# One unit of shares turned at a time, keys and values before queries, weight splits before the heads, and the latents' norms among the Hyena transforms

## The chip, the cores and the metric

The kernel runs on one core of one Trainium2 chip. The metric is the device time of one execution in microseconds (us); the median of several executions is given. The core has TensorE (PE, matmuls and transposes into PSUM), VectorE (DVE), ScalarE (ACT), GpSimd (POOL, here only an issuer of DMAs) and SyncE (SP, the issuer of the weight stream). Each engine works through its own queue in order and waits on semaphores.

## The reference

Two layers over 256 context and 256 latent tokens of width 1024. Each layer mixes tokens and then channels. Token mixing, cut to what matters here:

```python
hy, pool, cq, ckv, kpe = split(h @ w_in)          # 768, 256, 384, 256, 32 columns
y_hy   = hyena_mix(hy)                            # short convolution, long convolution by transforms, gates
y_pool = pool_mix(pool)                           # four window means, a 64x64 matmul for each group
k, v   = split(rmsnorm(ckv) @ w_ukv); k_pe = rope(kpe)
q      = rope(rmsnorm(cq) @ w_uq)                 # 8 heads of 64 + 32
att    = softmax(q @ k.T * SM_SCALE) @ v          # context sees context, latents see both
x      = x + gate * (concat(y_hy, y_pool, att) @ w_out)
```

Channel mixing is a dense SwiGLU in layer 0 and eight experts of SwiGLU, two for each token, in layer 1. In layer 1 only the latent tokens go on past the keys and values. All is float32; the large matmuls are made of three fp32r products of high and low parts.

## The kernel before, in words

Activations lie transposed, 128 channels by 512 tokens (256 context, 256 latent) in a tile. The order on each engine is written out by hand: PE, ACT, DVE, SP and POOL each have a program with a function for each stage (`project_in`, `hyena`, `pooling`, `latents`, `attention`, `project_out`), and all hand over through one counting semaphore for each engine (`pe_done`, `act_done`, `dve_done`); `after("name")` is the count at which a named step is done.

**Weight stream.** SP loads 1 MB granules in the order of `stream_plan()` into a ring of three `raw` buffers (a granule's load waits until the one three places before it has been used or split). For each granule ACT casts `w_hi` (L1102) and DVE subtracts `w_lo` (L1595), through `upto(g)` at places chosen by hand; there are three slots. Granules `("ada", 0, i)` hold modulation weights; PE uses them raw in `plain(n)` (two granules for each n), ACT saves the row (`save_row`), PE turns it (`turn`), DVE adds the bias (`bias_mod`). In layer 0 `plain(4)` to `plain(9)` are strewn through the mixing.

**Stages around the change, PE's order in layer 0.** `hyena`: transposes of z, eight matmuls against the transform bases (L617), `plain(4)` (in layer 1 `shift_rows`), wait for the products Y of DVE, inverse transform y (L630, L631). `pooling`: `turn(4)`, `plain(5)`, window matmuls d (L647), group matmuls yp (L656), with ACT's copies dT between. `latents`: `turn(5)`, `plain(6)`, transposes of the normed latents cq (L670) and ckv (L677) and of the rotary key (L683), `turn(6)`, `plain(7)`, the queries of eight heads (L695), keys (L703), values (L709), `turn(7)`, `plain(8)`. DVE computes the latents' sums of squares (L1849, L1852), the reciprocal (L1856), the scaling (L1860, L1863), the rotary key (L1870 to L1874), the drains of the queries (L1882 to L1891: one head is one PSUM bank, 256 context columns and 256 latent columns) and the copies of the values (L1895), in this order and behind all of Hyena. ACT drains the transposed latents (L1290, L1296), writes the rotary key into all heads' keys (L1301, eight copies) and drains the keys (L1309). POOL loads `w_uq`, `w_ukv` and both rotary tables in one go after the end of Hyena.

**Attention.** A unit is 128 query rows of one latent head against 512 keys, or one context head with both its query tiles against 256 keys. Layer 0 has 8 context and 16 latent units, layer 1 has 16 latent units. For each unit: PE scores (L728) into one of three banks; DVE maximum (L1908); ACT exponential with its sum (L1330) into one of four `prob` buffers; DVE reciprocal and scaling, the shares (L1917, L1921); PE transposes (L741); ACT copy to `probT` (L1345); for each pair of heads PE multiplies with the values (L755), ACT and DVE split the result (L1352, L1929). A latent head's `turn_p(n, half)` fills a bank with the blocks of one half of the keys for both query tiles, and so takes from both units of the head:

```python
for t in range(2):
    own = first[n] + t if s else u
    eng.wait_ge(dve_done, after(f"ps {l} {own}"))
```

Scores are issued three units ahead (`ahead_to(first[n] + half + 3)`). At heads `out_splits = {0: (4, 9, 12), 1: (1, 3, 5)}` ACT and DVE split the next granule of `w_out` inside the loop. `project_out` (L435 to L437) follows.

## Time and profile before

| | us |
|---|---|
| median of three runs | 1751.36 (1748.71 to 1754.73) |
| the profiled execution, its own time | 1748.31 |
| its span | 1746.5 |
| PE busy | 1631.9 (93%) |
| DVE busy | 1299.3 (74%) |
| ACT busy | 894.0 (51%) |
| share of the chain that ended last: PE, DVE, ACT | 63%, 16%, 5% |

The span is cut by the profile into 40 slices; the mixing of layer 0 lies in slices 3 to 7 (up to about 284 us, then its output projection), that of layer 1 in slices 18 to 21 (about 786 to 890 us). Busy time says how long an engine had work in flight, the chain says what the end waited for. The granted clock is TensorE's, as a share of 2.4 GHz; it has two levels, 1.2 and 2.4 GHz, and a stretch's figure is a mean over both.

### The profile page before, as it was taken

Reading aid. Unit: us, or ns where it says so; the run is one execution under the profiler, and the core shown is the slowest. Engines: PE = TensorE matmul, PEld = TensorE weight load, DVE = VectorE, ACT = ScalarE, POOL = GpSimd, SP = SyncE. Lnnn points to the kernel's source line nnn. Section 1 sums busy time; section 2 is a strip of 40 time slices with the busy share of each in tenths; the row PEclk is TensorE's granted clock in tenths of the full one; section 3 lists DMA queues with packets and bytes.
Section 4 is the critical chain, followed back from the end, with each engine's and each line's share of the span. In section 5 each row is a group of like instructions: output and inputs, shape, how many; then the busy total and the mean of one; then the engine's idle time right before and its main releaser. Section 6 shows DMA issues by size and latency. Waiting matters only on the chain.

```text
span 1746.5 us, 19442 instructions
## 1 busy us (share of the span) xinstructions
PE 1631.9 (93%) x7404; PEld 1269.4 (73%) x7404; DVE 1299.3 (74%) x1769; ACT 894.0 (51%) x1019; POOL 14.7 (1%) x31
## 2 busy tenths in 40 slices
PE   5998978899999999797888999999999999999996
PEld 3774446777888888685377778888787878878775
DVE  3825454688787765846447989898988989888897
ACT  3322264332222222432557776677777776777774
POOL 1000000000000000000000000000000000000000
PEclk8997999899999999898998999999999999999999
DMA  9225131354445553131026889899999999999993
GB/s 392 73 95 212 61 115 57 134 205 157 161 158 213 195 215 145 46 118 68 26 87 265 338 348 352 342 354 359 344 335 337 360 358 353 345 346 365 345 347 115
DMA packets 56004, 403.49 MB, mean 231 GB/s; under 512 B 6433, under 2 KB 6465, under 8 KB 8801
## 3 DMA queue, kind: packets, MB, share of 16 engines
q1 hardware_dynamic: 53712, 387.47, 59.1%
q0 software_dynamic: 2192, 14.70, 2.2%
q8 instruction: 62, 1.02, 0.2%
q14 instruction: 38, 0.30, 0.0%
HBM read 401.10 MB, written 1.05 MB: 230 GB/s over the span
## 4 chain that ended last, share of the span: by engine, by line
PE 63%; DVE 16%; ACT 5%; issue 3%; DVEq 0%; ACTq 0%
PE PS L435 18%; PE PS L437 18%; PE PS L436 18%; DVE w_lo L2234 5%; ACT w_hi L1472 3%; DVE w_lo L1595 1%; DVE arena L1608 1%; PE PS L986 1%; PE PS L728 1%; DVE small L1908 1%; PE PS L755 1%; DVE XT L1955 1%; DVE arena L1921 1%; DVE hT_lo L1743 1%; PE PS L741 1%
## 5 line engine op out<-in xcount | busy, mean ns | idle before, releaser
L2234 DVE TENSOR_TENSOR w_lo<-arena,w_hi 128x2048 fp32r<-128x2048 f32 x132 | 301.7, 2291 | 44.0 <-ACT w_hi L1472 44.0
L2234 DVE TENSOR_TENSOR w_lo<-raw,w_hi 128x2048 fp32r<-128x2048 f32 x129 | 295.0, 2291 | 32.7 <-ACT w_hi L1472 32.2
L1472 ACT CAST w_hi<-arena 128x2048 fp32r<-128x2048 f32 x132 | 251.6, 1909 | 47.3 <-PE PS L437 47.3
L1472 ACT CAST w_hi<-raw 128x2048 fp32r<-128x2048 f32 x129 | 246.9, 1916 | 44.3 <-PE PS L437 44.3
L435 PE MATMUL PS<-hT_hi,w_hi 128*128 128x512 f32 (+1 forms) x576 | 217.7, 378 | 11.3 <-DVE hT_lo L1743 9.9
L436 PE MATMUL PS<-hT_lo,w_hi 128*128 128x512 f32 (+1 forms) x576 | 214.8, 373 | 0.0
L437 PE MATMUL PS<-hT_hi,w_lo 128*128 128x512 f32 (+1 forms) x576 | 214.7, 373 | 0.0
L435 PE MATMUL PS<-w_hi,hT_hi 128*128 128x512 f32 (+1 forms) x448 | 178.3, 398 | 0.3 <-DVE w_lo L2234 0.3
L437 PE MATMUL PS<-w_hi,hT_lo 128*128 128x512 f32 (+1 forms) x448 | 174.6, 390 | 0.0
L436 PE MATMUL PS<-w_lo,hT_hi 128*128 128x512 f32 (+1 forms) x448 | 173.6, 388 | 0.0
L1595 DVE TENSOR_TENSOR w_lo<-raw,w_hi 128x2048 fp32r<-128x2048 f32 (+1 forms) x54 | 122.4, 2266 | 30.0 <-ACT w_hi L1102 29.9
L435 PE MATMUL PS<-w_hi,f_hi 128*128 128x512 f32 x352 | 140.6, 399 | 3.5 <-DVE f_lo L2241 3.5
L436 PE MATMUL PS<-w_lo,f_hi 128*128 128x512 f32 x352 | 139.0, 395 | 0.0
L437 PE MATMUL PS<-w_hi,f_lo 128*128 128x512 f32 x352 | 138.7, 394 | 0.0
L435 PEld LDWEIGHTS PS<-hT_hi,w_hi 128*128 128x128 f32 x576 | 110.6, 192 | 34.3 <-DVE hT_lo L1743 11.7
L435 PE MATMUL PS<-w_hi,odd_hi 128*128 128x512 f32 x336 | 135.3, 403 | 0.0
L1102 ACT CAST w_hi<-raw 128x2048 fp32r<-128x2048 f32 (+1 forms) x54 | 102.3, 1894 | 60.9 <-PE PS L437 53.3
L437 PE MATMUL PS<-w_hi,odd_lo 128*128 128x512 f32 x336 | 131.8, 392 | 0.0
L436 PE MATMUL PS<-w_lo,odd_hi 128*128 128x512 f32 x336 | 131.0, 390 | 0.0
L437 PEld LDWEIGHTS PS<-hT_hi,w_lo 128*128 128x128 f32 x576 | 110.5, 192 | 18.7
L436 PEld LDWEIGHTS PS<-hT_lo,w_hi 128*128 128x128 f32 x576 | 110.7, 192 | 18.1
L1955 DVE SCALAR_TENSOR_TENSOR XT<-PS,mod,XT 128x256 f32<-128x256 f32 x200 | 85.0, 477 | 40.3 <-PE PS L437 39.9
(320 smaller groups left out, 2533.3 us busy)
## 6 DMA issues: line engine op xcount, KB each, us to landing
raw<-in_moe SPq DMA_DIRECT2D x132, 1024.0 KB, 6.4
arena<-in_moe SPq DMA_DIRECT2D x132, 1024.0 KB, 6.6
raw<-in_ffn SPq DMA_DIRECT2D x33, 1024.0 KB, 4.8
raw<-in_dot SPq DMA_DIRECT2D x28, 1024.0 KB, 4.9
raw<-in_ada SPq DMA_DIRECT2D x17, 1024.0 KB, 6.7
raw<-in_out SPq DMA_DIRECT2D x8, 1024.0 KB, 4.8
raw<-in_inb SPq DMA_DIRECT2D x8, 960.0 KB, 4.8
raw<-in_ina SPq DMA_DIRECT2D x5, 1024.0 KB, 5.2
```

The costliest lines, as they stand in the source:

```text
L435: mm(out, s_hi, m_hi, start=start, stop=False)
L436: mm(out, s_hi, m_lo, start=False, stop=False)
L437: return mm(out, s_lo, m_hi, start=False, stop=stop)
L728: i = mm(o[:, q], qT[0:96, h, P * t:P * t + P], KT[0:96, h, 0:512 if s else 256], start=True, stop=True)
L741: i = nc.tensor.transpose(o[:, 256 * b + P * t:256 * b + P * t + P], prob[:, own % 4, at:at + P], ident[:, :])
L755: i = mm(o[VD * j:VD * j + VD, 0:256], V[:, b, VD * (h + j):VD * (h + j) + VD], probT[:, (2 * pair + j) % 4, b, :], start=b == 0, stop=b = ...
L986: last = nc.tensor.transpose(PS[:, 2, P * f:P * f + P], hh[:, s % 2, P * f:P * f + P], ident[:, :])
L1102: nc.scalar.copy(w_hi[:, slot[n], 0:w], raw_at(n)[:, 0:w]).then_inc(act_done, 1)
L1472: nc.scalar.copy(w_hi[:, x_slot(j), :], x_raw(n)).then_inc(x_hi, 1)
L1595: v.tensor_tensor(w_lo[:, slot[n], 0:w], raw_at(n)[:, 0:w], w_hi[:, slot[n], 0:w].bitcast(F32), ALU.subtract).then_inc(dve_done, 1)
L1955: v.scalar_tensor_tensor(out=XT[:, k, q], in0=o[:, q], scalar=mod[:, l, j + k, s:s + 1], in1=XT[:, k, q], op0=ALU.mult, op1=ALU.add).then_ ...
L2234: v.tensor_tensor(w_lo[:, x_slot(j), :], x_raw(NGR * (i % 2) + j), w_hi[:, x_slot(j), :].bitcast(F32), ALU.subtract).then_inc(x_lo, 1)
```

## The change

- PE, `hyena`: the window matmuls d move in front of the wait for Y. `pooling` starts with yp; `turn(4)` and `plain(5)` follow it.
- DVE, `hyena`: begins with `latent_sums` (sums of squares and the rotary key), then z times its bias; after Y comes `scale_latents`; both splits of Hyena's output come after both of its gates. ACT takes the square roots right after its copies of zT, and the splits' high parts after pooling's.
- PE, `latents`: ckv is turned before cq, `turn(5)` and `plain(6)` come after the transposes, then keys, values, queries. Queries are made in pairs of heads of one stream, one bank for a pair, 256 columns for each matmul instead of 512 in layer 0; DVE drains a context pair with one instruction and a latent pair with four 512 columns wide.
- The splits of three `w_out` granules leave the attention loop: ACT splits the first before the keys' drains and the next two after them, DVE the first before the values' copies and the others after query pairs 1 and 3. In the stream of layer 0 `("ada", 0, 16..19)` move behind the third of them.
- Attention: a unit is turned by itself, all its four blocks, as soon as its own shares are there; scores are issued four ahead; a `prob` buffer is free when its own unit was turned; `probT` is written in runs of 128.
- POOL: `w_ukv` is loaded once the forward transforms are done, `w_uq` and the query table once Hyena's gates are; the key table is loaded once.

```diff
@@ stream_plan
-            plan += [("ada", 0, i) for i in range(2 * BEFORE, 20)]
-        plan += [("out", l, i) for i in range(4)]
+            plan += [("ada", 0, i) for i in range(2 * BEFORE, 16)]
+        plan += [("out", l, i) for i in range(3)]
+        if l == 0:
+            plan += [("ada", 0, i) for i in range(16, 20)]
+        plan.append(("out", l, 3))
-        dT = A(2048, 2, 512)
+        dT = A(17544, 2, 512)
-        out_splits = {0: (4, 9, 12), 1: (1, 3, 5)}
@@ PE, latents
-                    turn(0, 5)
-                    plain(6)
+                for k in range(KKV):
+                    o = bank(f"ckvT {l} {k}")
...
                 if l == 0:
+                    turn(0, 5)
+                    plain(6)
                     turn(0, 6)
                     plain(7)
...
-                for h in range(HEADS):
-                    o = bank(f"q {l} {h}")
-                    for k in range(KQ):
-                        i = mm(o[:, sp], wuq[:, k, h, :], cqT[:, k, sp], start=k == 0, stop=k == KQ - 1)
...
+                heads = attention_plan(streams)[0]
+                for pair in range(len(heads) // 2):
+                    o = bank(f"q {l} {pair}", pair)
+                    for j in range(2):
+                        s, h = heads[2 * pair + j]
+                        for k in range(KQ):
+                            i = mm(o[:, 256 * j:256 * j + 256], wuq[:, k, h, :], cqT[:, k, 256 * s:256 * s + 256],
+                                   start=k == 0, stop=k == KQ - 1)
@@ PE, attention
-                def turn_p(n, half):
+                def turn_p(u):
+                    n, j = units[u]
                     s, h = heads[n]
-                    u = first[n] + half
+                    eng.wait_ge(dve_done, after(f"ps {l} {u}"))
                     o = bank(f"pT {l} {u}", 3 + u % 3)
-                    for t in range(2):
-                        own = first[n] + t if s else u
-                        eng.wait_ge(dve_done, after(f"ps {l} {own}"))
-                        for b in range(2):
-                            at = P * (2 * half + b) if s else 256 * t + P * b
-                            i = nc.tensor.transpose(o[:, 256 * b + P * t:256 * b + P * t + P],
-                                                    prob[:, own % 4, at:at + P], ident[:, :])
+                    for b in range(4):
+                        at = P * b if s else 256 * (b // 2) + P * (b % 2)
+                        to = P * b if s else 256 * (b % 2) + P * (b // 2)
+                        i = nc.tensor.transpose(o[:, to:to + P], prob[:, u % 4, at:at + P], ident[:, :])
...
-                ahead_to(2)
+                ahead_to(3)
...
-                        ahead_to(first[n] + half + 3)
-                        turn_p(n, half)
+                        ahead_to(first[n] + half + 4)
+                        turn_p(first[n] + half)
@@ ACT, latents
                 if l == 0:
                     save_row(0, 7)
+                upto(gindex[("out", l, 0, 0)])
                 for pr in range(4):
...
+                upto(gindex[("out", l, 2, 0)])
@@ ACT, attention
-                        m = units[u - 4][0]
-                        eng.wait_ge(pe_done, after(f"pT {l} {first[m] + heads[m][0]}"))
+                        eng.wait_ge(pe_done, after(f"pT {l} {u - 4}"))
...
-                    nc.scalar.copy(probT[:, n % 4, 2 * half:2 * half + 2, :],
-                                   bank_of(f"pT {l} {u}").rearrange("p (b q) -> p b q", q=256)).then_inc(act_done, 1)
+                    q = P if heads[n][0] else 256
+                    to = probT[:, n % 4, :, P * j:P * j + P] if heads[n][0] else probT[:, n % 4, 0:2, :]
+                    nc.scalar.copy(to, bank_of(f"pT {l} {u}").rearrange("p (b q) -> p b q", q=q)).then_inc(act_done, 1)
...
-                    if n in out_splits[l]:
-                        upto(gindex[("out", l, out_splits[l].index(n), 0)])
@@ DVE, new: latent_sums (first in hyena) and scale_latents (after Y), the instructions of latents before
+            def latent_sums(l, streams):
+                for t in range(NT):
+                    eng.wait_ge(act_done, after(f"Bs {l} 1 {t}"))
...
+                eng.wait_ge(*loaded["rope keys"])
...
+            def scale_latents(l, streams):
+                eng.wait_ge(act_done, after(f"stdq {l}"))
+                v.reciprocal(small[:, 24:32], small[:, 24:32]).then_inc(dve_done, 1)
...
@@ DVE, latents
+                upto(gindex[("out", l, 0, 0)])
                 for t in range(NT):
                     eng.wait_ge(pe_done, after(f"v {l} {t}"))
                     v.tensor_copy(V[:, t, :], bank_of(f"v {l} {t}")).then_inc(dve_done, 1)
...
+                for pair in range(len(heads) // 2):
+                    eng.wait_ge(pe_done, after(f"q {l} {pair}"))
+                    if heads[2 * pair][0] == 0:
+                        v.tensor_scalar(qT[0:96, pair, :], o[0:96, :], SM_SCALE, None, ALU.mult).then_inc(dve_done, 1)
...
+                    else:
+                        v.tensor_scalar(qT[0:64, pair, :], o[0:64, :], SM_SCALE, None, ALU.mult).then_inc(dve_done, 1)
+                        v.tensor_tensor(qT[64:96, pair, :], o[64:96, :], ropeq[64:96, :], ALU.mult).then_inc(dve_done, 1)
+                        v.tensor_tensor(qtmp[64:96, :], o[96:128, :], ropeq[96:128, :], ALU.mult).then_inc(dve_done, 1)
...
+                        v.tensor_tensor(qT[64:96, pair, :], qT[64:96, pair, :], qtmp[64:96, :], ALU.add).then_inc(dve_done, 1)
...
+                    if pair in (1, 3):
+                        upto(gindex[("out", l, 1 + pair // 2, 0)])
@@ POOL
-                eng.wait_ge(dve_done, after(f"hyena {l}"))
-                eng.wait_ge(pe_done, after(f"y {l} 1"))
+                if l == 0:
+                    load("rope keys", (A(20224, 128), io["ropek"]))
                 eng.wait_ge(pe_done, after(f"zT {l} 1"))
-                eng.wait_ge(act_done, after(f"mixhi {l} 1"))
-                load(f"mla {l}", (A(7936, 3072), io["wuq"][l]), (A(11008, 2048), io["wukv"][l]), (A(19712, 512), io["ropeq"]),
-                     (A(20224, 128), io["ropek"]))
+                eng.wait_ge(pe_done, after(f"Zs {l} 1"))
+                load(f"kv {l}", (A(11008, 2048), io["wukv"][l]))
+                eng.wait_ge(dve_done, after(f"yh {l} 1"))
+                load(f"q {l}", (A(7936, 3072), io["wuq"][l]), (A(19712, 512), io["ropeq"]))
```

## Rows read from the trace of the kernel before

**Rows 1.** The page's first part: busy time, share of the span, instructions.

```profile
PE 1631.9 (93%) x7404; PEld 1269.4 (73%) x7404; DVE 1299.3 (74%) x1769; ACT 894.0 (51%) x1019; POOL 14.7 (1%) x31
```

**Rows 2.** Stages: us; busy of PE, PEld, DVE, ACT, POOL; PEclk; DMA share; GB/s.

```profile
134.00:216.20 82.20, 75.50 (x290) 39.96 (x289) 38.83 (x105) 20.72 (x36) 2.16 (x4) 0.88 0.37 139
216.20:284.50 68.30, 53.23 (x285) 30.28 (x281) 39.82 (x92) 41.60 (x101) 0.00 (x0) 0.95 0.29 108
786.30:842.70 56.40, 45.46 (x171) 30.61 (x172) 29.80 (x82) 15.75 (x33) 2.14 (x4) 0.88 0.14 53
842.70:889.70 47.00, 35.19 (x162) 17.85 (x160) 28.34 (x55) 27.65 (x55) 2.11 (x4) 0.93 0.22 79
```

**Rows 3.** The chain that ended last, layer 1's attention: start, duration, engine and line.

```profile
857.54 1.81 ACT w_hi L1102
859.37 2.29 DVE w_lo L1595
861.66 0.60 DVE small L1908
...
877.03 0.69 DVE small L1908
877.83 0.50 DVE arena L1921
878.37 0.44 PE PS L741 x2
878.81 0.86 PE PS L728 x2
879.67 0.44 PE PS L741 x4
880.11 1.90 PE PS L755 x16
```

**Rows 4.** Groups by form, layer 1's mixing: busy, mean ns, idle before.

```profile
L1330 ACT ACTIVATE arena<-PS,small 128x512 f32<-128x512 f32 x16 | 11.0, 690 | 12.0 <-DVE small L1917 5.8 <-PE PS L755 5.6 <-issue 0.6
L695 PE MATMUL PS<-arena 128*128 128x256 f32 x48 | 11.6, 406 | 0.0
L695 PEld LDWEIGHTS PS<-arena 128*128 128x128 f32 x48 | 9.9, 209 | 1.6
L741 PE MATMUL PS<-ident,arena 128*128 128x128 f32 x64 | 12.1, 296 | 10.9 <-DVE arena L1921 10.9
L1301 ACT COPY arena<-PS 32x512 f32<-32x512 f32 x8 | 3.9, 579 | 0.2 <-PE PS L683 0.2
```

**Rows 5.** PE in order of time, layer 0: start, duration, idle before.

```profile
139.26 1.22 PE L630 MATMUL PS<-arena 128*128 128x256 f32 x2 [3.30 <-DVE arena L1808]
...
152.02 7.12 PE L647 MATMUL PS<-arena 128*64 128x256 f32 x32
...
169.96 3.87 PE L670 MATMUL PS<-ident,arena 128*128 128x128 f32 x12 [2.26 <-DVE arena L1860]
...
177.04 1.92 PE L445 MATMUL PS<-raw,cpad 128*32 128x512 f32 x16
```

**Rows 6.** PE in order of time, layer 1.

```profile
808.04 1.83 PE L670 MATMUL PS<-ident,arena 128*128 128x128 f32 x6 [5.92 <-DVE arena L1860]
...
827.18 8.80 PE L703 MATMUL PS<-arena 128*128 128x512 f32 x16 [3.35 <-DVE arena L1889]
```

**Rows 7.** DVE in order of time, both layers' first product Y, and a query drain.

```profile
130.78 0.42 DVE L1798 TENSOR_TENSOR arena<-PS,arena 128x256 f32<-128x256 f32 x1 [27.39 <-PE PS L617]
...
788.30 0.42 DVE L1798 TENSOR_TENSOR arena<-PS,arena 128x256 f32<-128x256 f32 x1 [19.85 <-PE PS L617]
...
815.25 0.42 DVE L1887 TENSOR_TENSOR arena<-PS,arena 32x256 f32<-32x256 f32 x1
```

**Rows 8.** DMA issues from 145 to 185 us: size, median time to landing.

```profile
raw<-in_ada SPq DMA_DIRECT2D x6, 1024.0 KB, 6.4
...
arena<-in_wukv POOLq DMA_DIRECT2D x1, 1024.0 KB, 12.1
```

More of the change, by code:

```diff
@@ L623, in hyena @@
                     shift_rows()
+                eng.wait_ge(*loaded[f"pool {l}"])
+                for t in tiles_of(streams):
+                    eng.wait_ge(act_done, after(f"Bs {l} 0 {t}"))
+                for g in range(4):
+                    o = bank(f"d {l} {g}")
+                    for s in streams:
+                        for t in range(2):
+                            i = mm(o[0:GROUP, 256 * s:256 * s + 256], Bm[:, 2 * s + t, GROUP * g:GROUP * g + GROUP],
+                                   pm[:, g, t, :], start=t == 0, stop=t == 1)
+                    i.then_inc(pe_done, 1)
+                    did(f"d {l} {g}")
                 eng.wait_ge(dve_done, after(f"Y {l}"))
@@ L635, in pooling @@
             def pooling(l, streams):
-                if l == 0:
-                    turn(0, 4)
-                    plain(5)
-                eng.wait_ge(*loaded[f"pool {l}"])
                 sp = span(streams)
-                for t in tiles_of(streams):
-                    eng.wait_ge(act_done, after(f"Bs {l} 0 {t}"))
-                for g in range(4):
-                    o = bank(f"d {l} {g}")
-                    for s in streams:
-                        for t in range(2):
-                            i = mm(o[0:GROUP, 256 * s:256 * s + 256], Bm[:, 2 * s + t, GROUP * g:GROUP * g + GROUP],
-                                   pm[:, g, t, :], start=t == 0, stop=t == 1)
-                    i.then_inc(pe_done, 1)
-                    did(f"d {l} {g}")
                 for pair in range(2):
@@ L1246, in hyena @@
                             did(f"zTs {l} {ct}", f"read zT {l} {ct}")
+                eng.wait_ge(dve_done, after(f"ssq {l}"))
+                act(small[:, 24:28], small[:, 16:20], ACT.Sqrt, bias=epsb[:, 0:1], scale=1.0 / QL).then_inc(act_done, 1)
+                did()
+                act(small[:, 28:32], small[:, 20:24], ACT.Sqrt, bias=epsb[:, 0:1], scale=1.0 / KVL).then_inc(act_done, 1)
+                did(f"stdq {l}")
                 if l == 0:
@@ L1253, in hyena @@
                         did("shift row", f"read shift {half}")
-                for ct in range(2):
-                    eng.wait_ge(dve_done, after(f"yh {l} {ct}"))
-                    nc.scalar.copy(hT_hi[:, ct, sp], ytmp[:, ct, sp]).then_inc(act_done, 1)
-                    did(f"mixhi {l} {ct}")
             def pooling(l, streams):
                 sp = span(streams)
-                if l == 0:
-                    save_row(0, 5)
                 for g in range(4):
@@ L1275, in pooling @@
                     did(f"mixhi {l} {2 + pair}")
+                for ct in range(2):
+                    eng.wait_ge(dve_done, after(f"yh {l} {ct}"))
+                    nc.scalar.copy(hT_hi[:, ct, sp], ytmp[:, ct, sp]).then_inc(act_done, 1)
+                    did(f"mixhi {l} {ct}")
+                if l == 0:
+                    save_row(0, 5)
             def latents(l, streams):
                 sp = span(streams)
[L1279 to L1283 removed]
                 if l == 0:
                     save_row(0, 6)
+                for k in range(KKV):
+                    eng.wait_ge(pe_done, after(f"ckvT {l} {k}"))
+                    o = bank_of(f"ckvT {l} {k}")
+                    a = PAR["kvg"][0] + k
+                    act(ckvT[:, k, :], o, ACT.Copy, scale=par[:, l, a:a + 1]).then_inc(act_done, 1)
+                    did(f"ckvTs {l} {k}", f"read ckvT {l} {k}")
                 for k in range(KQ):
@@ L1338, in soften_to, with save_turned @@
                         done += 1
-                def save_turned(n, half):
-                    u = first[n] + half
+                def save_turned(u):
+                    n, j = units[u]
                     eng.wait_ge(pe_done, after(f"pT {l} {u}"))
@@ L1357, in attention @@
                         soften_to(first[n] + half + 3)
-                        save_turned(n, half)
+                        save_turned(first[n] + half)
                     if l == 0 and n == 0:
@@ L1787, in hyena @@
             def hyena(l, streams):
                 sp = span(streams)
+                latent_sums(l, streams)
+                b0 = PAR["hyb"][0]
+                for ct in range(2):
+                    eng.wait_ge(pe_done, after(f"zT {l} {ct}"))
+                    z = uc[:, 2 + ct, sp]
+                    v.tensor_scalar(z, z, par[:, l, b0 + ct:b0 + ct + 1], None, ALU.mult).then_inc(dve_done, 1)
+                    did()
                 if l == 0:
```

157 lines of the change are left out of this document (67 added, 90 removed).

## The prediction

> **What bounds the kernel now.** I read the page first, then the stages around the change, then the chain, then single engines in order of time. PE is busy for 93% of the span [rows 1], but the mixing of both layers is where that is not so. From 134.0 to 216.2 us (layer 0, inverse transform to the first scores) PE is busy for 75.5 of 82.2 us at a mean clock of 0.88; in attention it is busy for 53.2 of 68.3; in layer 1 for 45.5 of 56.4 and for 35.2 of 47.0 [rows 2]. The reader is to see that neither DVE nor ACT fills those stretches (39.8 and 41.6 of 68.3, 28.3 and 27.7 of 47.0): they are bound by waits between engines, not by one engine. The chain says which: in layer 1's attention it runs maximum, share, transposes, score and round again, and through the two splits of a granule, 1.81 on ACT and then 2.29 on DVE [rows 3]. PE waited 10.9 us for shares before its transposes there [rows 4]. Ahead of attention PE waits for Y (3.30 us) and for the scaled latents (2.26 in layer 0, 5.92 in layer 1), and in layer 1 for the drain of the queries before the keys (3.35) [rows 5, 6].
>
> **Layer 0 ahead of attention.** A mean clock of 0.88 between the levels of 0.5 and 1 puts 24% of 82.2 us, 19.7 us, at the lower level. If the 6.7 idle us lie in it, 13.0 busy us ran at half speed and 6.5 were lost: the work at full clock is 69.0 us. The change removes none of it. It puts d, 7.1 us [rows 5], where the 3.30 us wait was. Y itself gets later: in front of it DVE now has six sums of squares for the queries and keys and more. But DVE sat idle for 27.39 us before Y [rows 7], and the last latent arrives less than 6 us before Y starts; I put the delay, with the key table's load, at 2.5 us, which 7.1 us of d cover (without them PE would wait 5.8). The scaled latents are ready before y ends, so the 2.26 us wait goes. The clock should then stay up. New waits: ACT's `save_row` 6 stands ahead of the drains of ckv, so `turn(6)` waits some 1.4 us for row and bank; and `plain(7)`'s second granule is loaded only when the first of `plain(6)` is used. A granule takes 6.4 us to land [rows 8]; between lie half of `plain(6)`, `turn(6)` with its wait, and half of `plain(7)` (1.9 us a `plain` [rows 5]), some 4.2 us: 2.2 us of waiting. The gap of 0.8 us in yp for ACT's copies stays. Sum: 69.0 + 1.4 + 2.2 + 0.8 = 73.4, a gain of 8.8; bounds 0 (the waits in ACT's queue give it all back) and 13.2 (no wait at all). The weights of the keys, 12.1 us to land [rows 8], are asked for about 35 us before their use, so their load is hidden; if it were not moved it would end the wait of the keys.
>
> **Queries in pairs.** In layer 0, 24 matmuls of 512 columns (two instructions each) become 48 of 256: as many columns, twice the weight loads. Layer 1 already does it so: 48 instructions of 256 columns in 11.6 us with 9.9 us of weight loads beside them [rows 4], a part of it at the lower clock. Loads and streams overlap there, so I price this at nothing; if they did not, 48 more loads at 0.209 us would be 10.0 us.
> The Trainium skill ("TensorE: Matmul & The Clock Gate", Part 3) says that a weight load overlaps a running matmul only where the row group differs, which speaks against this edit; by that rule queries in layer 1 should have taken the sum of both rows, 21.5 us, and they took 11.6, so the trace disagrees. By it the whole change would gain 10.0 us less.
>
> **Attention, layer 0.** PE's prices at full clock are 0.86 for a score, 0.44 for four transposes and 1.90 for the values of a latent pair, which is four units [rows 3]: 1.78 a unit, 28.4 for 16. A context unit has as many columns in its score and its turn and half as many value blocks: 1.78 too, 14.2 for 8. With `turn(8)` and `plain(9)` (about 2.8) that is 45.4 of the 68.3 us. The question is whether the other engines now let PE do it. DVE needs 0.60 to 0.69 for a maximum and 0.50 for a scaling; over layer 1's stretch (28.34 - 3 x 2.29) / 16 = 1.34 us a unit [rows 2, 3]. ACT needs (27.65 - 3 x 1.81) / 16 = 1.39. Both are under 1.78. The loop of waits is: exponential of u (0.69 and its sum), share (0.2 + 0.5), then the maximum of u+2 behind it in DVE's queue (0.6), then the exponential of u+2: some 2.4 us for two units, 1.2 a unit, also under 1.78. Before, `turn_p` of the first half waited for the share of the second unit, and the score that feeds the next pair stood behind it; now a unit waits for itself alone, with scores three further ahead and a `prob` buffer freed a unit earlier. The three splits, 3 x (1.81 + 2.29) of stalled queues [rows 3], leave the loop for a stretch in which PE is busy with values and queries and DVE for only a part. I add 0.9 us for the last share's way into the last value matmul, 1.3 us for `plain(9)`'s last granule, which now starts its load only when `plain(8)` begins, and 2.3 us of small gaps: 49.9 us, a gain of 18.4. Bounds: 0, and 22.9 (45.4 reached).
>
> **Layer 1 ahead of attention.** Of 56.4 us PE's full-clock work is between 38.7 and 44.2 (13.5 us at the lower level, with none or all of the 10.9 idle us in it [rows 2]); I take the middle, 41.5, plus 1 us, so the queries end at 828.8. DVE's sums again lie in its idle time before Y (19.85 us [rows 7]). The waits of 5.92 and 3.35 go. But what is late next is DVE: four query pairs, each 4 x 0.72 = 2.9 us (a 512-wide operation at 0.69 [rows 3]; a 256-wide one takes 0.42 [rows 7]), against 2.6 us a pair on PE, and two splits of 2.29 among them, the last right ahead of the first maximum. From the first pair on PE, 828.8 - 3 x 2.6 = 821.0, it is 11.6 + 4.6 = 16.2 us to the first maximum, 837.2, against 843.7 (the 842.7 of the stretch's end, one score and a handover later): 6.5 us earlier. PE waits for 8 us in between, and the wait will take its clock down for a while.
>
> **Attention, layer 1.** From the first maximum it is about 2.9 us to the first exponential's end. Three scores are done by then: 28.4 - 2.6 = 25.8 us of PE's work remain, plus 0.9 at the tail, 2.0 for the low clock after the wait (half of some 4 us), 1.5 of gaps: the last value matmul ends at 837.2 + 33.1 = 870.3 instead of 889.7, a gain of 19.4 for the layer, bounds 0 and 24. The output projections, the dense layer and the experts keep their work and order; their stalls are elsewhere. ACT's eight key copies (3.9 us [rows 4]) end before the third key matmul needs a bank; I price them at nothing.
>
> **Sum.** 8.8 + 18.4 + 19.4 = 46.6 us. I take off 2.6 for waits not foreseen: 44. The profiled execution took 1748.3 us (span 1746.5), so 1704.3; the median of the three runs is 3.1 above it: 1707.4.
>
> **Rivals.**
> 1. *The attention loop stays bound by handovers.* DVE and ACT are in order; a maximum queued behind a share that waits for ACT can make a unit take 2.3 us instead of 1.78 (against about 2.8 now). Then half of attention's 31.3 us (18.4 and 12.9) is had: gain 8.8 + 6.5 + 15.7 = 31 us, about 1720. For it: DVE waited for scores and ACT for maxima in the same stretch. Against: none of the loops adds up to 1.78. Chance 0.16.
> 2. *The queues ahead of attention take back what the order gives.* ACT's `save_row` 6 ahead of the ckv drains, the splits ahead of the values' copies, `plain` granules behind splits: the 15.3 us of both front stretches shrink to nothing: 31 us, about 1720. Chance 0.10.
> 3. *Weight loads show.* 48 more at 0.209 us, 10 us: 1717. Chance 0.04.
> 4. *Slower.* The copy into `probT` in runs of 128 (same 128x512 elements) would have to make ACT the bound: the 46.6 us of gain over 40 units, and the 1.78 us they are paced by, mean 2.9 us of ACT a unit, and so a copy of 2.1 us where a whole unit of ACT with its exponential now takes 1.39. From there on the change costs. No row shows such runs; 1755 to 1760 then. Chance 0.02.
> 5. *All waits gone*, over 54 us: under 1697. Chance 0.04.
> The forecast itself, 1697 to 1716, has 0.64.
>
> **Range.** Rivals 1 to 3 reach 1720 to 1726 (with half of 2 on top of 1); so 1697 to 1726. A measurement tells about 0.3%, 5 us, from no change: faster 0.95, same 0.02, slower 0.03.
>
> **What would show it.** In the profile after: PE without the wait before L630 and the clock near 1 up to the queries; the L741 group's idle time before it down from 10.9 us to 3 or less in layer 1; no L1102 or L1595 between L1908s; score starts 1.8 us apart; in layer 1 an idle PE of some 8 us after the third score. It would be wrong if L741 still waits for L1921 in every unit, if ACT's L1345 grew beyond 0.6 us, or if PE waits for a granule at `plain(7)` to `plain(9)` for more than a few us.

## The result, and the profile after

| | us |
|---|---|
| before, median of four runs | 1751.71 (1748.71 to 1754.73) |
| changed kernel, median of four runs | 1708.59 (1707.65 to 1709.24) |
| ratio, 95% interval | 0.9755 (0.9739 to 0.977) |
| predicted | 1707.4, range 1697 to 1726 |
| profiled execution after, its span | 1708.7, 1706.8 |

The medians differ by 43.1 us, the profiled executions by 39.6; that of before lies 3.4 us under its own median, which is the rest. The stages below are read against the 39.6.

Line numbers below are those of the kernel profiled, so one step has other numbers after than in [rows] and in some experiments. The page after, its first part and the engines of the chain that ended last; they answer to [rows 1]:

```profile
PE 1618.1 (95%) x7452; PEld 1273.2 (75%) x7452; DVE 1294.3 (76%) x1733; ACT 891.7 (52%) x1019; POOL 14.1 (1%) x30
...
PE 76%; DVE 15%; ACT 5%; issue 3%; DMA 1%; SPq 0%; DVEq 0%; ACTq 0%
```

PE is busy for 14 us less although it runs 48 instructions more: less of its work fell into time at half the clock (the mean granted clock of the two profiled executions is 0.977 against 0.97). Its share of the chain grew from 63% to 76%, so the waits were what went. The same stages as in [rows 2] (up to the first score, and attention; columns as there):

```profile
134.80:210.60 75.80, 71.16 (x337) 44.96 (x336) 37.32 (x65) 23.62 (x36) 1.60 (x3) 0.93 0.51 191
210.60:259.20 48.60, 47.31 (x284) 29.70 (x280) 34.89 (x93) 35.36 (x98) 0.00 (x0) 1.00 0.22 87
761.70:808.00 46.30, 42.40 (x171) 28.22 (x172) 23.91 (x51) 20.69 (x36) 1.62 (x3) 0.96 0.24 86
808.00:850.20 42.20, 32.65 (x162) 18.28 (x160) 29.41 (x61) 22.02 (x52) 2.12 (x4) 0.84 0.14 53
```

In layer 0 the front went from 82.2 to 75.8 us and attention from 68.3 to 48.6, where PE is now busy for 97% at a clock of 1.00. In layer 1 the front is 10.1 us shorter up to the first score, but attention only 4.8: a wait moved over the border. From the first maximum on, the split that I used, the front gained 2.6 us and attention 12.4.

PE in order of time, layer 0's front (start, duration, idle before):

```profile
136.67 7.12 PE L635 MATMUL PS<-arena 128*64 128x256 f32 x32
143.72 0.70 PE L645 MATMUL PS<-arena 128*128 128x256 f32 x2
...
164.01 1.94 PE L449 MATMUL PS<-raw,cpad 128*32 128x512 f32 x8 [2.45 <-DMA raw<-in_ada]
167.33 1.84 PE L469 MATMUL PS<-sel,rows 128*128 128x2 f32 x8 [1.39 <-ACT arena L1296]
169.10 3.64 PE L449 MATMUL PS<-raw,cpad 128*32 128x512 f32 x16
```

The window matmuls (L635) run straight into y (L645): the 3.30 us wait of [rows 5] is gone. The two waits behind them are the granule and `turn(6)`, and what runs after them is at half speed: 16 of L449 took 3.64 us where they take 1.92 at full clock. DVE in front of Y, which had idled for 27.39 us there [rows 7], now waits 5.13 us for the key table; by these rows that wait, and not the sums of squares, is what makes Y later:

```profile
131.79 0.19 DVE L1809 TENSOR_TENSOR arena<-arena 128x32 f32<-128x32 f32 x1 [5.13 <-DMA arena<-in_ropek]
...
133.45 0.42 DVE L1848 TENSOR_TENSOR arena<-PS,arena 128x256 f32<-128x256 f32 x1
```

Groups by form, the queries of layer 0:

```profile
L716 PE MATMUL PS<-arena 128*128 128x256 f32 x96 | 20.9, 379 | 0.0
...
L716 PEld LDWEIGHTS PS<-arena 128*128 128x128 f32 x96 | 18.2, 190 | 2.9 <-issue 0.5
```

96 instructions with 18.2 us of weight loads beside them in 20.9 us; before, 48 of 512 columns took 20.87 (all of L695 in layer 0). Groups by form, attention of layer 0 and then, last two rows, the mixing of layer 1, against L741 in [rows 4]:

```profile
L749 PE MATMUL PS<-ident,arena 128*128 128x128 f32 x96 | 14.2, 273 | 0.0
L1356 ACT COPY arena<-PS 128x512 f32<-128x512 f32 x24 | 14.1, 593 | 8.8 <-PE PS L749 8.7
...
L737 PE MATMUL PS<-arena 96*128 96x512 f32 x32 | 19.0, 684 | 8.6 <-ACT arena L1339 7.7 <-DVE arena L1913 0.9
...
L749 PE MATMUL PS<-ident,arena 128*128 128x128 f32 x64 | 10.3, 291 | 0.0
```

No transposes wait for shares any more. The copy in runs of 128 takes 0.59 us. What is left in layer 1 is one idle of 7.7 us ahead of the fourth score. PE and then DVE in order of time there, against [rows 6, 7]:

```profile
779.93 1.96 PE L698 MATMUL PS<-arena 128*128 128x512 f32 x4 [1.40 <-ACT arena L1302]
783.80 7.12 PE L698 MATMUL PS<-arena 128*128 128x512 f32 x12 [1.91 <-ACT arena L1309]
...
819.57 2.04 PE L737 MATMUL PS<-arena 96*128 96x512 f32 x2 [7.70 <-ACT arena L1339]
```
```profile
792.67 0.69 DVE L1899 COPY arena<-PS 128x512 f32<-128x512 f32 x1 [4.67 <-PE PS L704]
...
800.41 0.68 DVE L1909 TENSOR_SCALAR arena<-PS 64x512 f32<-64x512 f32 x1 [1.90 <-PE PS L716]
...
806.17 2.29 DVE L1603 TENSOR_TENSOR w_lo<-raw,w_hi 128x2048 fp32r<-128x2048 f32 x1
...
814.26 2.29 DVE L1603 TENSOR_TENSOR w_lo<-raw,w_hi 128x2048 fp32r<-128x2048 f32 x1
816.58 1.29 DVE L1930 TENSOR_REDUCE small<-PS 128x1 f32<-128x512 f32 x2
```

The reader is to see three things: the keys wait for ACT twice; DVE idles for 4.67 us and more ahead of the query drains (L1909); and then it makes two splits (L1603) in the one stretch where everyone waits for it. The three experiments on mends below follow from these rows.

### The profile page after: what moved, and what is told of

It reads as the page before. It is cut to its first block, busy times and chain, and to the rows that moved or that the text cites. A ratio compares the mean times of both kernels' runs of the same rounds, so it can differ in the third digit from the quotient of the medians.

```text
span 1706.8 us, 19495 instructions
## 1 busy us (share of the span) xinstructions
PE 1618.1 (95%) x7452; PEld 1273.2 (75%) x7452; DVE 1294.3 (76%) x1733; ACT 891.7 (52%) x1019; POOL 14.1 (1%) x30
## 3 DMA queue, kind: packets, MB, share of 16 engines
HBM read 401.03 MB, written 1.05 MB: 236 GB/s over the span
## 4 chain that ended last, share of the span: by engine, by line
PE 76%; DVE 15%; ACT 5%; issue 3%; DMA 1%; SPq 0%; DVEq 0%; ACTq 0%
PE PS L439 20%; PE PS L441 20%; PE PS L440 20%; DVE w_lo L2254 6%; ACT w_hi L1480 3%; PE PS L737 2%; DVE arena L1616 1%; DVE w_lo L1603 1%; PE PS L993 1%; PE PS L762 1%; PE PS L749 1%; DMA arena<-in_ada 1%; PE PS L698 1%; PE PS L449 1%; PE PS L704 1%
## 5 line engine op out<-in xcount | busy, mean ns | idle before, releaser
L439 PE MATMUL PS<-hT_hi,w_hi 128*128 128x512 f32 (+1 forms) x576 | 217.6, 378 | 12.2 <-DVE hT_lo L1751 10.6
L1603 DVE TENSOR_TENSOR w_lo<-raw,w_hi 128x2048 fp32r<-128x2048 f32 (+1 forms) x54 | 122.3, 2266 | 34.8 <-ACT w_hi L1109 34.6
L439 PEld LDWEIGHTS PS<-hT_hi,w_hi 128*128 128x128 f32 x576 | 110.3, 191 | 34.7 <-DVE hT_lo L1751 12.4
```

Of the source, the lines that this page charges most:

```text
L439: mm(out, s_hi, m_hi, start=start, stop=False)
L1603: v.tensor_tensor(w_lo[:, slot[n], 0:w], raw_at(n)[:, 0:w], w_hi[:, slot[n], 0:w].bitcast(F32), ALU.subtract).then_inc(dve_done, 1)
```

## The experiments

Each was timed against the kernel before, whose medians in the four series were 1750.8, 1751.4, 1751.0 and 1751.4 us. "Layer 0 attention" is from the first score to the last value matmul's start, "layer 1" from the first transform to there; the changed kernel has 48.3 and 88.2 there, the kernel before 68.0 and 102.9. All stages are from one profiled execution each. In layer 1 twelve key matmuls, behind the same wait of 1.91 us, took 7.12 us in the profiles marked * and 5.42 in those marked + (last section); compare that column within a group, or take 1.7 us off the marked *.

| run | median, us | ratio (95%) | layer 0 attention | layer 1 |
|---|---|---|---|---|
| changed kernel | 1708.59 | 0.9755 (0.9739 to 0.977) | 48.3 | 88.2 * |
| halves, three ahead | 1730.58 | 0.9884 (0.9866 to 0.9902) | 61.2 | 95.2 + |
| splits inside | 1720.80 | 0.9831 (0.9815 to 0.9848) | 56.7 | 89.1 + |
| both | 1736.81 | 0.9917 (0.9897 to 0.9937) | 69.5 | 96.0 + |
| three ahead | 1717.10 | 0.9807 (0.9791 to 0.9824) | 53.8 | 89.9 * |
| halves, four ahead | 1709.38 | 0.9766 (0.975 to 0.9782) | 48.6 | 88.3 * |
| before + unit turning, four ahead | 1730.90 | 0.9889 (0.9873 to 0.9906) | 56.6 | 94.3 |
| before + four ahead | 1736.70 | 0.9918 (0.9902 to 0.9935) | 60.2 | 99.0 |
| windows behind y | 1713.91 | 0.9784 (0.9766 to 0.9801) | 48.3 | 88.6 * |
| splits among the values | 1702.57 | 0.9723 (0.9706 to 0.9741) | 48.3 | 81.7 + |
| key banks | 1705.18 | 0.9734 (0.9712 to 0.9757) | 48.3 | 82.3 |
| layer 0's front | 1705.10 | 0.9738 (0.9719 to 0.9756) | 48.3 | 85.9 + |
| all mends | 1698.95 | 0.9699 (0.9681 to 0.9718) | 51.1 | 78.7 |

### Which part of the change made the loop fast

**1. Halves, three ahead.**

```diff
-                    eng.wait_ge(dve_done, after(f"ps {l} {u}"))
+                    for t in range(2):
+                        own = first[n] + t if s else u
+                        eng.wait_ge(dve_done, after(f"ps {l} {own}"))
...
-                        ahead_to(first[n] + half + 4)
-                        turn_p(first[n] + half)
+                        ahead_to(first[n] + half + 3)
+                        turn_p(n, half)
```

> The changed kernel with the turning of the shares taken back alone: turn_p(n, half) fills a bank from both units of a latent head and waits for both shares, probT is written in runs of 256, a prob buffer is free only when the whole head was turned, scores are three units ahead. Keys and values first, the splits ahead of the heads and the mixing's order stay as changed. Theory (the wait for the second share makes the loop, and splits come on top of it): the larger part of attention's gain goes, some 12 us in layer 0 and 7 in layer 1, so about 1727; the transposes' idle time before them comes back in every head. Rival S (the splits in the loop were the stall, 3 x (1.81 + 2.29) = 12.3 us a layer): less than 5 us slower, up to 1713.

22.0 us slower; layer 0's attention is 13.0 us longer and layer 1 7.0 (8.7 with the keys at the same clock): near the theory's 12 and 7. PE there, for two heads (L750 are the transposes, L764 the values):

```profile
248.64 1.95 PE L764 MATMUL PS<-arena 128*64 128x256 f32 x16
...
253.02 0.44 PE L750 MATMUL PS<-ident,arena 128*128 128x128 f32 x2 [1.16 <-DVE arena L1945]
...
256.99 0.44 PE L750 MATMUL PS<-ident,arena 128*128 128x128 f32 x2 [0.80 <-DVE arena L1945]
...
258.66 1.95 PE L764 MATMUL PS<-arena 128*64 128x256 f32 x16
```

The second block of each head waits for the second unit's share: 10.02 us for four units.

**2. Splits inside the loop**, the stream's order of before with them.

```diff
+        out_splits = {0: (4, 9, 12), 1: (1, 3, 5)}
...
-                upto(gindex[("out", l, 0, 0)])
...
+                    if n in out_splits[l]:
+                        upto(gindex[("out", l, out_splits[l].index(n), 0)])
```

> The changed kernel with the three splits of w_out in each layer back inside the attention loop (and the stream's order of before, which goes with them); turning by the unit and everything else stay. Theory: each split holds ACT for 1.81 us and then DVE for 2.29, but with scores four ahead a part of it is covered: 2 to 3 us a split in the loop, less the 2 us that the DVE splits cost ahead of layer 1's first maximum; 8 to 12 us slower in all, 1717 to 1721. Rival S: 24.6 us less about 4 in front, so about 1729. Rival C (with per-unit turning the splits are covered by PE's own 1.78 us a unit): within 3 us of the changed kernel, or faster through layer 1's front.

12.2 us slower, at the edge of what the theory gave. In layer 0 the three splits cost attention 8.5 us. In layer 1 they cost 7.3 after the first maximum, but that maximum comes 48.5 us after the first transform instead of 54.9, so the layer as a whole differs by 0.9 us. Of the 6.3 us of the maximum 1.7 are the clock of the keys; with that taken off, the maximum moves by the 4.6 of two splits and the layer differs by 2.6. Out of the loop, most of what layer 1's splits cost had only been moved ahead of it.

**3. Both back.**

> The changed kernel with both taken back, turning by halves with scores three ahead and the splits inside the loop; keys and values first, queries in pairs and the mixing's order stay. Theory: all of attention's gain of 32 us goes and layer 1's front gains 2 to 4 by the splits it no longer holds: about 1738. If the two parts of the gain are separate causes, this is the sum of the two runs with one taken back; if each is enough to keep the loop slow, it is less than the sum.

28.2 us slower, against a sum of 34.2 for the two alone (the edit is both diffs above). In layer 0's attention they are separate causes (13.0 + 8.5 us; together 21.3). Of the 6.0 us by which the sum is missed a part lies ahead of attention: up to the first score layer 0 is 2.9 us shorter than in the changed kernel, against 0.0 and 0.7 in the two runs before. Why, and where the rest lies, was not found. Attention in layer 0 takes 69.5 us with both back, 68.0 before: queries in pairs and the rest of the change gave it nothing. This run is still 14.0 us faster than the kernel before, and that comes from the fronts: up to the first maximum layer 0 is 9.0 us shorter than before and layer 1 8.9.

**4. Three ahead**, turning by the unit.

```diff
-                ahead_to(3)
+                ahead_to(2)
...
-                        ahead_to(first[n] + half + 4)
+                        ahead_to(first[n] + half + 3)
```

> The changed kernel with scores three units ahead instead of four (ahead_to(2), then + 3); turning stays by the unit. Theory (the depth only hides jitter, the gain is in what turn_p waits for): 1 to 4 us slower, 1710 to 1713. Rival D (the depth carries the gain): over 10 us slower, since a unit's round through maximum, exponential and share is some 2.9 us and PE has 1.78 us of work a unit to put in front of it.

8.5 us slower, twice the theory's bound and under the rival's. So the depth is more than jitter.

**5. Halves, four ahead.** Experiment 1 with `ahead_to(3)` and `+ 4` left as they are in the changed kernel.

> The changed kernel with the turning by halves back, as in the first experiment, but scores four units ahead as changed. Taken back together they cost 22.0 us, the depth alone 8.5. Theory (each hides a part of the same round of maximum, exponential and share): turning alone costs 10 to 15 us, 1719 to 1724. Rival (where a half waits for the second unit's share, a fourth score ahead can't be used): as with three ahead, 1729 to 1731.

0.8 us slower than the changed kernel, which these measurements can't tell from no change. Both the theory and the rival were wrong: with a fourth score ahead it hardly matters whether a unit or a half is turned. One round of layer 0's loop, from one value group to the next (four units), takes in the four runs: 7.27 us as changed, 7.35 halves and four ahead, 7.86 units and three ahead, 10.02 halves and three ahead. Start times of the changed kernel (L762 the values, L737 a score):

```profile
239.74 1.95 PE L762 MATMUL PS<-arena 128*64 128x256 f32 x16
241.62 1.12 PE L737 MATMUL PS<-arena 96*128 96x512 f32 x2
242.58 0.60 PE L749 MATMUL PS<-ident,arena 128*128 128x128 f32 x4
...
247.01 1.95 PE L762 MATMUL PS<-arena 128*64 128x256 f32 x16
```

The programs say why: DVE takes the maximum of unit u+1 ahead of the share of unit u. With halves, the first transposes of a head need the share of u+1 and therefore the score of u+2. Three ahead, that is the last score issued, directly in front of them; four ahead, there is one more score between (0.86 us of PE), and units instead of halves give one more again. The count of scores between fits the two ends, none (10.02) and two (7.27). It doesn't explain the middle: both others have one, and one of them costs 8.5 us, the other 0.8. A half waits only once for two units, a unit each time; that this makes the difference was not tested.

**6. Unit turning and four ahead on the kernel before; 7. four ahead alone on it.**

> The kernel before with one part of the change alone: turn_p by the unit, scores four ahead, prob buffers freed by the unit, probT in runs of 128. Splits stay in the loop, queries ahead of keys, mixing as before. Theory (the parts act in the attention loop and nowhere else, so they give what they gave between the runs with both taken back and with the splits inside alone, 1736.8 - 1720.8 = 16.0): 16 us faster than the kernel before, about 1735. Rival (the gain depends on what stands ahead of attention): under 8 us.

> The kernel before with nothing changed but the depth: ahead_to(3) and + 4. Turning stays by halves, the splits in the loop, queries ahead of keys. Theory (DVE takes the maximum of unit u + 1 ahead of the share of unit u, so the first half of a head, which needs the share of u + 1, needs the score of u + 2, and with three ahead that is the last one issued, right in front of the transposes; a fourth score is work for PE in that wait): nearly all of what unit turning and depth gave together on this kernel (20.1 us), 15 to 20 us, 1731 to 1736. Rival (the depth suffices only where the splits are out of the loop): under 10 us, above 1741.

```diff
-                ahead_to(2)
+                ahead_to(3)
...
-                        ahead_to(first[n] + half + 3)
+                        ahead_to(first[n] + half + 4)
```

The diff is that of experiment 7; experiment 6 has it and the turning, the copy and the freeing of the `prob` buffers as changed. They are 20.1 us and 14.7 us faster than before. The first was expected at 16: on this kernel the parts give more. The two numbers in the source, 3 and 4, are by themselves worth a third of the whole change; unit turning adds 5.4 where the splits still stall the loop, 0.8 where they don't. In the last run PE still waits, at longer distances:

```profile
254.50 1.13 PE L728 MATMUL PS<-arena 96*128 96x512 f32 x2
256.37 0.41 PE L741 MATMUL PS<-ident,arena 128*128 128x128 f32 x2 [0.75 <-DVE arena L1921]
```

14.7 is just outside the 15 to 20 expected.

### The fronts

Of what the change did ahead of attention, only the place of the window matmuls was taken back alone. That the waits for the scaled latents (2.26 and 5.92 us) and for the queries' drains (3.35) of [rows 5, 6] are gone is read from the trace after; what keys before queries, the earlier sums and the earlier loads give each by themselves was not run.

**8. Windows behind y**, and ACT's high parts of Hyena's output back ahead of pooling's copies.

```diff
@@ PE, hyena
-                for g in range(4):
-                    o = bank(f"d {l} {g}")
...
@@ PE, pooling
+                if l == 0:
+                    turn(0, 4)
+                    plain(5)
+                for g in range(4):
+                    o = bank(f"d {l} {g}")
```

> The changed kernel with the window matmuls d put back behind y in both layers, turn(4) and plain(5) back in front of them, and the high parts of Hyena's output back ahead of pooling's copies on ACT; the sums of the latents stay ahead of Y. Theory (d is the cover of Y's delay): in layer 0 PE stands idle for Y, by the 3.30 us of before and the 1.9 that Y now starts later after the transforms, some 5 us and a lower clock after it; in layer 1, where d is 3.7 us, some 2 to 4 us. All of it passes on to the end: 7 to 11 us slower, 1716 to 1720. Rival (what is late next in the front takes it up, the granule of plain(6) in layer 0 and DVE's queue in layer 1): at most 4 us slower.

5.3 us slower, between the two. PE waits for Y in layer 0 by the predicted amount (L634 is y here), and the first ten matmuls of y then run at half speed:

```profile
144.54 1.22 PE L634 MATMUL PS<-arena 128*128 128x256 f32 x2 [5.29 <-DVE arena L1859]
```

But the granule of `plain(6)` is no longer late and that of `plain(7)` by 0.66 only: of 5.29 us of wait 3.1 reach the first score. In layer 1 Y waits 1.04 us and the layer differs by 0.4. The rival was right about that half. 1.8 us of the 5.3 lie outside both stages and are not explained.

**9. Splits among the values**, layer 1 alone.

```diff
-                upto(gindex[("out", l, 0, 0)])
+                upto(gindex[("out", l, l, 0)])
                 for t in range(NT):
...
+                    if l and t == 1:
+                        upto(gindex[("out", l, 2, 0)])
```

> The changed kernel with another place for two splits in layer 1 alone: ACT makes the high parts of the first two granules ahead of the keys' drains, DVE their low parts ahead of the values' copies and the third one's after the second value copy, where it has gaps of 4.7 and 1.0 us; none stands among the query pairs or ahead of the first maximum. Layer 0 is as changed. Theory (the two splits among the pairs push the first maximum by their own length and more: 54.9 us after the transforms' start here, 48.5 where they were inside the loop): the first maximum comes 4.5 to 6 us earlier, attention after it stays at 33 to 35 us, 3.5 to 6 us faster: 1703 to 1705. Rival (PE is the bound after the queries, its idle 7.7 us is only moved into the loop): within 2 us of the changed kernel.

6.0 us faster, the upper end of what the theory gave. In the profiles layer 1 is 6.5 us shorter, of which the two splits are 4.6 and the clock of the keys 1.7; against splits inside the loop (experiment 2, keys at the same clock) it is 7.4 us shorter. DVE with the splits in its gaps, the last drains, and the maximum 48.5 us after the first transform, where splits inside the loop had put it too:

```profile
785.01 4.49 DVE L1603 TENSOR_TENSOR w_lo<-raw,w_hi 128x2048 fp32r<-128x2048 f32 x2 [6.83 <-ACT w_hi L1109]
...
793.34 2.29 DVE L1603 TENSOR_TENSOR w_lo<-raw,w_hi 128x2048 fp32r<-128x2048 f32 x1 [0.65 <-ACT w_hi L1109]
...
809.55 1.29 DVE L1932 TENSOR_REDUCE small<-PS 128x1 f32<-128x512 f32 x2
```

**10. Key banks**, layer 1.

```diff
-                    o = bank(f"k {l} {pr}", pr)
+                    o = bank(f"k {l} {pr}", (pr + 2 * l) % 4)
```

> The changed kernel with the keys of layer 1 in other banks: the first two pairs in 2 and 3, the last two in 0 and 1, where the third query latent and the rotary key are still to be drained. Theory (the waits of 1.40 and 1.91 us ahead of the keys are for these two banks, and all behind them follows from PE): both waits go, the low clock after them too, 3 to 5 us faster: 1703 to 1706. Rival (ACT, which has eight rotary copies, a split and eight key drains to do, is late for the scores, or DVE's splits hold the first maximum anyway): no change.

3.4 us faster. The two waits (3.31 us) became one of 0.42, and all sixteen run at full clock. Up to the first score layer 1 is 4.9 us shorter than in the changed kernel's profile and 3.2 shorter than in profiles with the same waits and the keys at full clock (experiment 11); the waits alone would account for nearly all of the 3.4:

```profile
778.07 7.10 PE L698 MATMUL PS<-arena 128*128 128x512 f32 x16 [0.42 <-DVE hT_lo L1885]
```

**11. Layer 0's front.**

```diff
+                if l == 0:
+                    eng.wait_ge(pe_done, after(f"used {gindex[('ada', 0, 12, 0)]}"))
                 load(f"q {l}", (A(7936, 3072), io["wuq"][l]), (A(19712, 512), io["ropeq"]))
```

and `save_row(0, 6)` behind the drains of both latents.

> The changed kernel with two edits in layer 0 alone: the load of the query weights (1.5 MB and 0.25) waits until plain(6)'s first granule has been used, so that it doesn't run beside the granules of plain(6), and ACT drains the latents before it saves row 6. Theory (plain(6)'s second granule lands late because it shares the DMA engines, and turn(6) waits for a drain that stands behind save_row(6)): the 2.45 us and half of the 1.39 us go and the clock stays up until the keys, 3 to 6 us faster: 1703 to 1706. Rival (the granule is late because its place in the ring came free late): the wait stays, under 1.5 us faster. If the query weights become the wait, PE stands idle ahead of the queries and it is slower.

3.5 us faster; in the profile the stretch up to the first score is 4.4 us shorter. The waits of 2.45 and 1.39 became these:

```profile
165.61 1.05 PE L469 MATMUL PS<-sel,rows 128*128 128x2 f32 x8 [0.70 <-ACT rows L1128]
...
169.03 1.94 PE L449 MATMUL PS<-raw,cpad 128*32 128x512 f32 x8 [1.37 <-DMA raw<-in_ada]
```

1.8 us of it is wait, the rest the clock: L469 takes 1.05 us instead of 1.84. Both edits were made at once; what each gave was not run. The granule of `plain(6)` is in time when the query weights don't load beside it; the queue has only moved, to `plain(7)`. How much of it is the ring and how much the bandwidth was not separated.

**12. All mends** of 9 to 11, and three more:

```diff
@@ ACT, latents
+                if l:
+                    upto(gindex[("out", l, 0, 0)])
                 for h in range(HEADS):
                     nc.scalar.copy(KT[64:96, h, :], o[0:ROPE, :]).then_inc(act_done, 1)
...
+                act(small[:, 249:250], small[:, 250:251], ACT.Exp).then_inc(act_done, 1)
@@ DVE, attention
                         largest(u)
                     if u == 0:
+                        drain_queries(l, len(heads) // 2 - 1)
```

> The changed kernel with the mends of the sixth, seventh and eighth experiments together (6.0, 3.4 and 3.5 us faster one by one), and three more: in layer 1 the first granule's high part ahead of the rotary key's copies, the last query pair drained only after the first maximum, and an exponential of one column on ACT ahead of attention, so that its table is loaded (1.28 us in the rows) before the first maximum is there. Theory: the three add up, 12.9 us, and the first maximum of layer 1 comes 4 us earlier still, of which PE, whose work from the queries' end on is now the bound, lets 1 to 3 through: 1693 to 1695. Rival (each mend takes from the same idle time of PE in layer 1): 1699 to 1702.

1698.95 us, 9.6 faster than the changed kernel and 52 than before, but 4 short of the expectation and at the rival's bound. In layer 0 one `plain` ahead of attention ran at half clock (3.62 us instead of 1.92), and attention grew from 48.3 to 51.1: the drain held back holds a bank that `turn(8)` wants (1.19 us), and a lower clock follows. In layer 1 the high part pushes the rotary copies, and the drained pair stands between the first two maxima (DVE):

```profile
788.10 1.98 PE L698 MATMUL PS<-arena 128*128 128x512 f32 x4 [1.25 <-ACT arena L1311]
...
813.51 1.11 PE L749 MATMUL PS<-ident,arena 128*128 128x128 f32 x4 [2.13 <-DVE arena L1953]
```
```profile
808.57 0.69 DVE L1940 TENSOR_REDUCE small<-PS 128x1 f32<-128x512 f32 x1
...
812.05 0.69 DVE L1940 TENSOR_REDUCE small<-PS 128x1 f32<-128x512 f32 x1
```

In layer 0 the extras cost attention 2.8 us. The first three mends without them were not run together, so what the extras give or cost in all, and how far the three mends add up, is not shown. This is the fastest version measured.

## Why the prediction was right, and where its steps were not

The time, 1707.4 against 1708.59, is nearer than its terms were, and part of that is luck: the profiled execution was to gain 44.0 us and gained 39.6. The 3.1 us that I added because the profiled execution of before lay under its median made up for most of the difference; the changed kernel's lies 0.1 us from its median.

| term | predicted gain | measured |
|---|---|---|
| layer 0 ahead of attention | 8.8 | 6.3 |
| layer 0 attention | 18.4 | 19.7 |
| layer 1 up to the first maximum | 6.5 | 2.6 |
| layer 1 attention | 12.9 | 12.4 |
| not foreseen, elsewhere | -2.6 | -1.4 (39.6 less the four) |

**Layer 0's front.** The rows bear out each wait: 2.45 us for a granule (2.2, though at `plain(6)`, one earlier than I put it), 1.39 for `turn(6)` (1.4), 0.8 in yp. Y came 1.9 us later after the transforms (2.5), through the key table's load, and d covered it. Wrong was "the clock should then stay up": it fell after those waits. The last term of my sum was the full-clock work, 69.0; nothing was set aside for the clock, and 2.5 us are missing. Experiment 11 has them back with the waits.

**Queries in pairs.** Nothing, as priced; rival 3 is out: 18.2 us of loads lie beside 20.9 us of matmuls, for the sum of both PE would have needed 39. The rule of the Trainium skill ("TensorE: Matmul & The Clock Gate", Part 3) that only loads of another row group overlap does not hold here; the same section also names a background weight buffer into which loads go ahead, and with that the trace agrees.

**Layer 0's attention.** 1.78 us a unit by the durations; 1.82 measured, with gaps of 0.36 and 0.93 at either end. Rival 1 is out here, rival 4 too (0.59 us a copy). The time of this stretch came out, the reason given was only half right. I named both "now a unit waits for itself alone" and "with scores three further ahead" and weighed them as one. Experiments 1, 4 and 5 weigh them: the wait for the second unit's share was the loop's bound, one more score in front takes away 21.2 of the 22.0 us by itself, and turning by the unit alone 13.5. The depth is the larger of the two. That the splits stalled the loop beside it held, 8.5 us of 21.3.

**Layer 1's front.** The failed step is "ACT's eight key copies end before the third key matmul needs a bank; I price them at nothing". They held a bank of the second and the cq drains that of the first pair: 3.31 us of wait and, in this profile, 1.7 of low clock; experiment 10 gets 3.4 back. The first query pair was ready 38.7 us after the transforms' start, not 34.7. From there on the count of drains and two splits, 16.2 us, measured 16.17. The idle PE of 8 us was 7.7. So the mechanism was right, and what I had not asked was whether those splits could stand where DVE idles: that was worth another 6.0 (experiment 9).

**Layer 1's attention.** 33.1 us from the first maximum, 33.6 measured.

**Rival 2** came about in part: 6.4 of the 15.3 us of both fronts were taken back, by the queues it named and by the clock. One bound of mine was added up wrongly: rival 1's 1720 with half of rival 2's 15.3 us is 1728, not 1726.

## What to carry to other kernels

Ahead of any reordering, count for the first wait of a loop how many units lie between what it needs and the last one issued, the other engines' in-order queues included; if it is none, try one more issue ahead first (14.7 of 20.1 us on the kernel before, 21.2 of 22.0 on the changed one, two numbers in the source). Work taken out of a loop is gained only if it lands where its engine idles: three splits ahead of the first maximum gave 2.6 us in layer 1 with the keys at the same clock, the same three among the value copies 7.4. A small wait of PE costs its own length and can cost the clock behind it; a bank whose reader does eight copies is such a wait.

## What the runs showed of the hardware

- The clock after like waits is not the same in each execution. The twelve key matmuls of layer 1 behind the same 1.40 and 1.91 us of idle took 7.12 us in the changed kernel (above) and 5.42 in experiment 1. Nine kernels have the 1.91 us wait there: the changed one and experiments 4, 5 and 8 took 7.1 us, experiments 1, 2, 3, 9 and 11 5.4. What else differs between them has not been found; a profile's stage can differ by 1.7 us for this alone. In experiment 1:

```profile
798.39 5.42 PE L698 MATMUL PS<-arena 128*128 128x512 f32 x12 [1.91 <-ACT arena L1311]
```

- In layer 0 the first transform starts near 127.5 us in some profiled executions and near 130.2 in others, whatever was edited behind it, and the layer 1 column of experiment 11, which edits layer 0 alone, is 2.3 us under the changed kernel's, 1.7 of it these keys. So stages were read from their own first transform, and they don't add up to the medians better than by such amounts.
- The first exponential of an attention pays for a table, on the path: in the changed kernel ACT idled 21.62 us for the first maximum and only then loaded it.

```profile
817.35 1.28 ACT L1339 ACT_TABLE_LOAD   x1 [21.62 <-DVE small L1930]
818.65 0.69 ACT L1339 ACTIVATE arena<-PS,small 128x512 f32<-128x512 f32 x1
```

The exponential starts 0.02 us after the load's end. The Trainium skill ("ScalarE activation tables: per-element evaluation and per-set limits", What a function is on this engine) gives 1283 ns for such a load, and the trace agrees. In experiment 12 a single-column exponential moved it to 796.51, out of the way; what that alone is worth was not run.
